# Band biases in natural order added by VectorE, and TensorE's work reordered in two attentions

## The reference, cut to what matters

```python
# first attention: 8 heads, causal
s = jnp.where(k_pos[None, :] <= q_pos[:, None], q @ k.T * scale, NEG_INF); out = softmax(s) @ v
# second ("attention 2"): 12 heads in three groups, a band bias for each head, and 4 heads over a memory
logits = jnp.where(valid, q @ k.T + bias_band, NEG_INF_2)
m = jnp.max(logits, -1); p = jnp.exp(logits - m[..., None]); den = jnp.sum(p, -1)
wts = softmax over the three groups of (m + jnp.log(den)); mixed = concat(p @ v / den * wts)
mem_out = softmax(q_mem @ k_mem.T * scale) @ v_mem
out = concat([mixed, mem_out]) @ w_out
```

## Time and profile before

| | |
|---|---|
| three timed runs, median (lowest to highest) | 2144.69 us (2143.53 to 2150.32) |
| the profiled execution's own time | 2137.23 us |
| its span in the profile | 2135.1 us |
| TensorE matmul, busy | 1900.5 us (89%) |
| VectorE, busy | 585.2 us (27%) |
| ScalarE, busy | 409.5 us (19%) |
| mean granted clock of TensorE | 0.956 |
| transfers | 574.46 MB, mean 269 GB/s |

### The profile page before, as it was taken

The page is one execution under the profiler, slowest core; times in us unless marked ns, Lnnn a source line. Parts: engine busy times, 40 slices in busy tenths (PEclk is TensorE's granted clock), DMA queues, the critical chain, the costliest instruction groups (busy, mean ns, idle before and its releaser), DMA issues.

```text
span 2135.1 us, 24595 instructions
## 1 busy us (share of the span) xinstructions
PE 1900.5 (89%) x9841; PEld 1054.0 (49%) x9842; DVE 585.2 (27%) x1155; ACT 409.5 (19%) x596; POOL 60.9 (3%) x82
## 2 busy tenths in 40 slices
PE   6989997899998887889788779989999999999998
PEld 4645452233332222223232238558884677768863
DVE  4657242211222111212222122331000289520001
ACT  2220222121212122112211221120000334220000
POOL 2000010000000000000000010003001000000000
PEclk9999998999999899999999889999999999999999
DMA  9654758999999999999999992084440423074420
GB/s 317 230 187 171 263 205 354 427 427 391 419 428 428 428 428 427 428 420 390 428 428 428 428 399 102 0 306 130 144 150 22 140 79 129 1 286 149 141 84 20
DMA packets 106225, 574.46 MB, mean 269 GB/s; under 512 B 7271, under 2 KB 8803, under 8 KB 81552
## 3 DMA queue, kind: packets, MB, share of 16 engines
q1 hardware_dynamic: 102000, 563.46, 66.0%
q0 software_dynamic: 4160, 10.06, 1.7%
HBM read 572.42 MB, written 1.07 MB: 269 GB/s over the span
## 4 chain that ended last, share of the span: by engine, by line
PE 72%; DMA 15%; DVE 5%; ACT 4%; issue 2%; SPq 1%; DVEq 0%; ACTq 0%
DMA ring<-in_w_up 14%; PE ps L2073 13%; PE ps L1468 10%; PE ps L2079 7%; PE ps L1503 5%; PE ps L711 5%; PE ps L1482 3%; PE ps L1515 3%; PE ps L897 2%; PE ps L1492 2%; PE ps L2052 2%; PE ps L2175 1%; PE ps L2601 1%; PE ps L1022 1%; DMA ring<-in_w_in 1%
## 5 line engine op out<-in xcount | busy, mean ns | idle before, releaser
L2073 PE MATMUL ps<-arena,ring 128*128 128x256 f32 x1280 | 276.6, 379 | 0.0
L2073 PEld LDWEIGHTS ps<-arena,ring 128*128 128x128 f32 x1280 | 243.6, 190 | 32.4
L1503 PE MATMUL ps<-ring,arena 128*32 128x512 f32 x1216 | 164.5, 690 | 62.1 <-DMA ring<-in_w_up 62.0
L1468 PE MATMUL ps<-ring,arena 128*64 128x512 f32 x960 | 213.1, 596 | 0.0
L2079 PE MATMUL ps<-ring,arena 128*128 128x512 f32 x352 | 151.4, 592 | 0.0
L711 PE MATMUL ps<-arena,ring 128*128 128x256 f32 x608 | 132.8, 380 | 0.0
L1468 PEld LDWEIGHTS ps<-ring,arena 128*64 128x64 f32 x960 | 66.2, 137 | 134.2 <-issue 133.9
L1503 PEld LDWEIGHTS ps<-ring,arena 128*32 128x32 f32 x1216 | 39.8, 125 | 173.4 <-issue 102.6
L711 PEld LDWEIGHTS ps<-arena,ring 128*128 128x128 f32 x608 | 115.3, 190 | 16.7 <-issue 1.6
L1482 PE MATMUL ps<-ring,arena 128*64 128x512 f32 x480 | 106.3, 595 | 11.2 <-ACT arena L1431 11.2
L2079 PEld LDWEIGHTS ps<-ring,arena 128*128 128x128 f32 x352 | 67.0, 190 | 83.2 <-issue 83.1
(11 more groups left out here) (615 smaller groups left out, 2069.8 us busy)
## 6 DMA issues: line engine op xcount, KB each, us to landing
ring<-in_w_gate SPq DMA_DIRECT2D x64, 2048.0 KB, 19.2
ring<-in_w_up SPq DMA_DIRECT2D x64, 2048.0 KB, 22.1
ring<-in_w_down SPq DMA_DIRECT2D x64, 2048.0 KB, 20.3
ring<-in_ffn_w_gate_up SPq DMA_DIRECT2D x22, 2048.0 KB, 8.6
ring<-in_ada_w SPq DMA_DIRECT2D x12, 2048.0 KB, 12.6
ring<-in_ffn_w_down SPq DMA_DIRECT2D x10, 2048.0 KB, 8.0
ring<-in_w_in SPq DMA_DIRECT2D x8, 2048.0 KB, 21.7
ring<-in_dn_w_in SPq DMA_DIRECT2D x6, 2048.0 KB, 7.8
```

The lines of the kernel that those rows point to most:

```text
L1468: m = pe.matmul(bank(b)[c * CAP:(c + 1) * CAP, :], xT[:, j * P + h * CAP:j * P + (h + 1) * CAP], w[h][:, j, c * 512:(c + 1) * 512], start= ...
L1503: m = pe.matmul(bank(b)[(2 * i + c) * FEW:(2 * i + c + 1) * FEW, :], xT[:, j * P + h * CAP:j * P + h * CAP + FEW], w[h][:, j, c * 512:(c + ...
L2073: m = pe.matmul(bank(b0 + g)[:, c * SEQ:(c + 1) * SEQ], w[:, k, (2 * g + c) * P:(2 * g + c + 1) * P], hT2[:, k, :], start=(k == 0), stop=( ...
```

## The change

**Biases.** SyncE copies `band_bias` to a new DRAM tensor `band_rows`, each head's row 128 times. Read with a step of one row less one value, it gives every query its window in natural order, so no flip is needed. VectorE scales the scores and adds the bias (`added`), then takes the maximum and its negative (`top`); ScalarE subtracts it as the bias of its exponential, one head at a time, and sums in the same pass. VectorE's sum goes away. Units 9 to 11 and their banks are interleaved with the rest by hand, and the memory values stand between the scores.

**First attention.** Scores run two units ahead, inside the wait for ScalarE's copy (`meanwhile`); gate 2 comes ahead of the conditioning rows, these stand in unit 2's wait, and the first drive in unit 3's.

**Memory units.** Both are transposed, into different banks, ahead of both value groups.

```diff
+        def sp_bias_rows(sp):
+            sp.wait_ge(bv_stored, 16 * 3)
+            src = bass.AP(bv_dram.tensor, bv_dram.offset, [[2 * SEQ, ATT_HEADS], [0, P], [1, 2 * SEQ]])
+            sp.dma_start(bv_rows, src).then_inc(sp_stored, 16)
...
         def sp_s7(sp):
             for i in range(SLOTS):
                 used = pieces[FIRST - SLOTS + i]
+                if i == SLOTS - 1:
+                    sp_bias_rows(sp)
                 sp.wait_ge(used[1], used[2])
                 load_in(sp, i, 0)
...
         def pool_s9(pool):
             pool.wait_ge(pos_ready, 1)
+            pool.wait_ge(sp_stored, 16)
...
-                        src = bass.AP(bv_dram.tensor, bv_dram.offset + (HPG * g + a) * 2 * SEQ + SEQ - (t + 1) * P,
-                                      [[1, P], [2 * 2 * SEQ, 2], [1, SEQ]])
+                        src = bass.AP(bv_rows.tensor, bv_rows.offset + (HPG * g + a) * P * 2 * SEQ + SEQ - 1 - t * P,
+                                      [[2 * SEQ - 1, P], [2 * P * 2 * SEQ, 2], [1, SEQ]])
...
-                for a in range(2):
-                    pe.matmul(bank(2 * (u % 2) + a), con("flip"), bias[:, 2 * a:2 * a + 2, :], start=True, stop=False, skip_group_check=True)
...
-        def pe_probs(pe, u, n, v_of):
+        def pe_probs(pe, u, n, v_of, meanwhile=lambda: None):
...
             m.then_inc(prT_ps, 1)
+            meanwhile()
             pe.wait_ge(prT_ready, n + 1)
...
+            def late_rows():
+                pe.wait_ge(gate_ready, 3)
+                pe_ada2(pe, 0, 7)
             scores(0)
+            scores(1)
             for u, (g, t) in enumerate(U1):
-                if u + 1 < len(U1):
-                    scores(u + 1)
...
-                if u == 2:
-                    pe_ada2(pe, 0, 7)
-                else:
-                    pe_gate(pe, min(u, 2), 7)
-                pe_probs(pe, u, u, lambda kb, i: vN[:, kb, (HPG * g + i) * HD:(HPG * g + i + 1) * HD])
+                if u < 3:
+                    pe_gate(pe, u, 7)
+                pe_probs(pe, u, u, lambda kb, i: vN[:, kb, (HPG * g + i) * HD:(HPG * g + i + 1) * HD], (late_rows, before_values)[u - 2] if u > 1 else
+                         lambda: scores(u + 2))
...
-        def pe_mem_probs(pe, i):
-            for t in range(TT):
-                pe_probs(pe, MU[i] + t, MU[i] + t, lambda kb, i_: vm[:, kb, i_ * HD:(i_ + 1) * HD])
+        def pe_mem_probs(pe):
+            for n in (4, 5):
+                pe_probs_turned(pe, n, turned_bank(n), 1)
+            for n in (4, 5):
+                pe_probs_values(pe, n, lambda kb, i_: vm[:, kb, i_ * HD:(i_ + 1) * HD])
...
+        def score_bank(n):
+            return 0 if n == 11 else 2 * (n % 2)
+        def turned_bank(n):
+            return 4 - 2 * (n % 2)
...
+            for n in (6, 7, 8):
+                scores(n)
+            pe_mem_values(pe, 1, 5, 0)
+            scores(9)
+            pe_mem_values(pe, 1, 5, 1)
+            scores(10)
+            scores(11)
...
+            turn(6)
+            turn(7)
+            values(6)
+            turn(8)
+            values(7)
+            values(8)
+            ws = [arrived(pe, pc) for pc in pc_ao[0]]
+            pe.wait_ge(ps_read, SQ + 6)
+            pe.wait_ge(pv_ev, 9)
+            out_of(0, 0, 0, KD)
+            turn(9)
+            out_of(0, 1, 0, KD).then_inc(first_ps, 1)
+            turn(10)
+            values(9)
+            turn(11)
+            values(10)
+            values(11)
             pe.wait_ge(pv_ev, 12)
...
+            def exps_less_top(n):
...
+                for h in range(HPG):
+                    o(act.activation(s3[:, h, :], s3[:, h, :], ACT.Exp, bias=nmx[t][:, g, h:h + 1], accum_out=dn3[t][:, g, h:h + 1]),
+                      sc_exp if h == HPG - 1 else None)
...
-                for g in range(3):
-                    n = 6 + 3 * t + g
-                    dve.wait_ge(sc_exp, n + 1)
-                    o(dve.tensor_reduce(dn3[t][:, g, :], heads(n), AX.X, ALU.add))
+                dve.wait_ge(sc_exp, 9 + 3 * t)
                 dve.wait_ge(fn_done, t + 2)
...
+                o(dve.scalar_tensor_tensor(heads(n), bank(score_bank(n), 2).rearrange("p (h k) -> p h k", h=HPG), HD ** -0.5, BM[t][g],
+                                           ALU.mult, ALU.add), ps_read)
+            def top(n):
+                t, g = (n - 6) // 3, (n - 6) % 3
+                o(dve.tensor_reduce(mx3[t][:, g, :], heads(n), AX.X, ALU.max))
+                o(dve.tensor_scalar(nmx[t][:, g, :], mx3[t][:, g, :], -1.0, None, ALU.mult), sc_sub)
...
+            added(6)
+            added(7)
+            top(6)
+            added(8)
+            top(7)
+            top(8)
+            tops(0)
+            added(9)
+            top(9)
+            added(10)
+            weigh(0)
+            top(10)
+            added(11)
+            top(11)
+            tops(1)
+            outs(0)
+            weigh(1)
+            outs(1)
```

More of the change, by code:

```diff
@@ L58, in shape_constants @@
     c["zero_rows"] = np.zeros((P, P))
-    c["flip"] = np.eye(P)[::-1] * HD ** 0.5
     half = HD // 2
@@ L802, in probs_of, with pe_scores @@
             return prob6[n - 6] if 6 <= n < 12 else prob[n % 2]
-        def pe_scores(pe, u, q_of, k_of, bias=None):
-            if bias is not None:
-                for a in range(2):
-                    pe.matmul(bank(2 * (u % 2) + a), con("flip"), bias[:, 2 * a:2 * a + 2, :], start=True, stop=False, skip_group_check=True)
+        def pe_scores(pe, u, q_of, k_of, b0=None):
+            if b0 is None:
+                b0 = 2 * (u % 2)
             for i in range(HPG):
-                m = pe.matmul(bank(2 * (u % 2) + i % 2)[:, (i // 2) * SEQ:(i // 2 + 1) * SEQ], q_of(i), k_of(i), start=bias is None, stop=True,
-                              skip_group_check=bias is not None)
+                m = pe.matmul(bank(b0 + i % 2)[:, (i // 2) * SEQ:(i // 2 + 1) * SEQ], q_of(i), k_of(i), start=True, stop=True)
             m.then_inc(sc_ps, 1)
@@ L874, in act_probsT @@
                 act.wait_ge(pv_ps, n - 1)
-            o(act.copy(prT[n % 2], bank(4, 2)), prT_ready)
+            o(act.copy(prT[n % 2], bank(b0, 2)), prT_ready)
         U1 = [(g, t) for g in range(HEADS // HPG) for t in range(TT)]
@@ L954, in gate_bank, with pe_drive @@
             return 4 + (i + 1) % 2
[L956 to L972 removed]
+        def pe_drive(pe, q):
+            if q:
+                pe.wait_ge(ps_read, q)
+            else:
+                pe.wait_ge(sc_sub, len(U1))
+            for n, (now, last) in enumerate(((BTr, BLr), (BTi, BLi))):
+                at_ = n * HALF
+                for j in range(4):
+                    pe.matmul(bank(j)[:, at_:at_ + HALF], now[32 * j:32 * j + 32, q, :],
+                              uT[32 * j:32 * j + 32, q, :].rearrange("p (s r) -> p r s", r=2)[:, 0, :],
+                              start=True, stop=False, tile_position=(32 * j, 0), skip_group_check=True)
+                for j in range(4):
+                    m = pe.matmul(bank(j)[:, at_ + 1:at_ + HALF], last[32 * j:32 * j + 32, q, :],
+                                  uT[32 * j:32 * j + 32, q, :].rearrange("p (s r) -> p r s", r=2)[:, 1, 0:HALF - 1],
+                                  start=False, stop=True, tile_position=(32 * j, 0), skip_group_check=True)
+            m.then_inc(bu_ps, 1)
+        def pe_s3(pe):
             def gate(i):
@@ L994, in y_of @@
                 m.then_inc(y_ps, 1)
-            drive(0)
             gate(3)
-            drive(1)
+            pe.wait_ge(pv_ev, len(U1))
+            pe.wait_ge(mod_read, 5)
+            pe_drive(pe, 1)
             gate(4)
             y_of(0)
-            drive(2)
+            pe_drive(pe, 2)
             gate(5)
             y_of(1)
-            drive(3)
+            pe_drive(pe, 3)
             gate(6)
@@ L2016, in block_kernel @@
         mxx = [ar(9216 + 40 * t + 36, HPG) for t in range(TT)]
+        nmx = [ar3(9296 + 12 * t, 12, 3) for t in range(TT)]
         actF = ar3(10240, FC2 * SEQ, FC2)
@@ L2177, in out_of, with turn, values @@
                 return m
-            for g in range(3):
-                pe_probs(pe, 6 + g, 6 + g, values_of(g))
-            for g, part in enumerate(((0, 0, KD), (1, 0, KD // 2), (1, KD // 2, KD))):
-                pe_probs_turned(pe, 9 + g)
-                if g == 0:
-                    ws = [arrived(pe, pc) for pc in pc_ao[0]]
-                    pe.wait_ge(pv_ev, 9)
-                    pe.wait_ge(sc_sub, 12)
-                m = out_of(0, *part)
-                if g == 2:
-                    m.then_inc(first_ps, 1)
-                pe_probs_values(pe, 9 + g, values_of(g))
+            def turn(n):
+                if n == 7:
+                    pe.wait_ge(ps_read, SQ + 4)
+                pe_probs_turned(pe, n, turned_bank(n), 1)
+            def values(n):
+                pe_probs_values(pe, n, values_of((n - 6) % 3))
+            turn(6)
[15 more added lines that the diff above has]
+            values(11)
```

(2 more changed lines are left out.)

114 lines of the change are left out of this document (52 added, 62 removed).

## The result

The changed kernel has a median of **2122.7 us** (2112.33 to 2124.36, four runs), against 2147.48 (2143.53 to 2150.32, four runs) for the kernel before: a ratio of 0.9879, 95% interval [0.9852, 0.9905]. It is 25 us faster by the medians, 26 by the ratio; 2120.8 were predicted. Measured again as an experiment it gave the same ratio, 0.9879 [0.9863, 0.9894].

A forecast was written before the change was run, and what follows sets the result against it. TensorE carries 72% of the chain and transfers of expert weights 15%, so waits removed from TensorE outside the experts shorten the run. 10.3 + 2.2 + 11.4 = 23.9 us off the median 2144.69 gives 2120.8; range 2112 to 2133.

The forecast's parts named there:

- First attention, 10.3 us: First attention: regrouped TensorE work starts gate 3 at 147.9 instead of 158.43 us; 10.3 us after 0.2 for handovers.
- It reaches the end: Up to the experts no transfer is on the chain; the expert stream starts and ends 10.3 us sooner.
- The prediction's own sign of being wrong: Wrong if last experts' end to first feed-forward isn't 13 to 14 us shorter, or experts 1, 2 wait longer for weights.
- The copy at nothing: First expert's loads: the 3.15 MB DRAM copy, 8.2 us at 385 GB/s, hides in 16 us of free transfer engines.
- one engine, 131 us: Rival: the copy runs on one transfer engine of 16 at 24 GB/s, 131 us, ending at 2236; chance 0.03.
- Memory units, 2.2 us: Memory units: both transposes first, second values at once behind the first; end 1330.7 instead of 1332.92, 2.2 us.
- Band units, 11.4 us: Attention 2: the output projection's second tile starts at 1412.5 instead of 1423.94 us, 11.4 us sooner.
- The projection starts there: Output projection: starts at 1389.9 us, when both output weights have landed, 16.2 us after the memory values end at 1373.7.
- The low clock: Output projection: its first records run at the lower clock after a sparse stretch, costing 1.7 us (8.77 less 7.07).
- unit 8's copy stands behind unit 10's exponentials on ScalarE: Attention 2: unit 8's copy waits until 1384.7 and takes 1.0 us more; its values end at 1387.
- TensorE waits there for VectorE: Kernel before, 1392 to 1400 us, ahead of the output projection: TensorE waits while VectorE sums and weighs every unit.
- The base: Whole run: the 23.9 us are taken off the timed median, 2144.69, giving 2120.8; off the profiled 2137.23, 2113.3.

The follow-up runs named there:

- four copies: Kernel before with the copy of the bias rows made four times, unused: 2166.86 us against 2145.16, ratio 1.0098.

## Why the prediction was right

**First attention, 10.3 us: right, 10.7.** Both causes were as put: the other work fills the waits for copies, and the conditioning weights are there in time, so that the rows run at 7.07 us.

**It reaches the end: right, by the timed runs.** Alone the first attention gave 11.2 us of the run, 8.4 to 14.2. From the second expert's first issue to the end of the stream are 910.4 to 915.0 us in the thirteen profiles without four copies, 911.8 before, so the stream adds or takes up to 3 us of its own. Ahead of it the clock hides part of the gain in a single profile: gate 3 to that issue took 167.5 to 171.9 us in the five with the old first attention and 169.2 to 175.3 in the eight with the new. Whether the new order makes the low clock there more frequent is not decided. The prediction's own sign of being wrong did not come: from the last expert's last group (1261.18 before, 1261.00 after) to the first feed-forward (1437.78, 1424.29) are 13.3 us less, and between 320 and 440 us TensorE waits for weights for 3.6 us, 4.4 before.

**The copy at nothing: right, with the wrong rate.** I took 385 GB/s and 8.2 us; it runs at 306 GB/s for 10.3 us. Both fit the gap of 16 us. (The 10.3 is 3.15 MB at 306 GB/s; the copy's landing is in no view.) A share of 0.79 where full loads show 1.02 to 1.04 is 0.77 of theirs, near 12 engines of 16 (0.75); which engines carried it no view shows. The Trainium skill (DMA: Bandwidth & Descriptors, Rules for kernel authors) says that an outermost dimension below 16 confines a DMA to at most that many engines. By that the copy was estimated at 10.9 us, and the trace agrees with it rather than with 8.2. The rival "one engine, 131 us" was a rate that no run showed.

**Memory units, 2.2 us: right in their stretch, 2.26.** Timed alone they gave 4.7 us, 2.4 to 7.1, so perhaps more than their stretch; where the rest came from is not shown (above).

**Band units, 11.4 us: right, 11.2 and 11.1** in the two profiles of the changed kernel (62.04 less 50.81 and less 50.98). The step that carried the number, "The projection starts there" at the landing of the output weights, held: 16.5 us behind the issue (16.2 said), waiting for a transfer. The low clock cost 1.6 us where 1.7 stood, priced from another place; in the five profiles with the 2.30 us hold it cost 1.5 to 2.3, so the close agreement is partly luck.

**What was wrong in it did not matter for the sum.** "unit 8's copy stands behind unit 10's exponentials on ScalarE" is true, but the second holder, VectorE's read of unit 6 out of the bank that unit 8's values need, was missed. I had VectorE's passes up to the weighing and its read of unit 8, but put the reads of units 6 and 7 nowhere. ScalarE's unit was 2.53 us and not 2.35: 510 ns for 256 columns from on-chip memory where I took 474 from a row that reads PSUM. Both errors lay under the weights' landing, with 1.5 us of slack. And "TensorE waits there for VectorE", of the 17 us ahead of the projection in the kernel before, holds for the first wait alone, 2.43 us until unit 6 is weighed; the three behind it, 1.14 to 1.15 each, were for ScalarE's copies, and four of the short groups took twice their time at the low clock. No term of the sum rests on it.

**The base: right.** The sum of 23.9 was taken off the median, 2144.69, and not off the profiled execution. The profiled pair shows only 13 us, since the profiled execution of before was early: its unit 0 began at 104.59, those of all other profiles at 105.5 to 110.2. And the way from there to the second expert's first issue differs by the clock too: 327.63 - 104.59 = 223.0 us before, 325.85 - 107.36 = 218.5 after, 4.5 us apart where 10.7 were spared; in 240 to 330 us the clock was 0.92 in the one and 0.85 in the other. Over the profiles this way takes 221.7 to 227.4 us with the old first attention (five, without that of four copies) and 212.3 to 218.5 with the new (eight): the one before is the second shortest of its kind, the one after among the longest.

**Do the parts add up?** First attention 10.7, memory units 2.3, band units 11.2: 24.2 us, for 26.0 measured, 22.7 to 29.4. The parts timed alone add up to more, 11.2 + 4.7 + 14.2 = 30.1; each is uncertain by 2 to 3 us, so the 4 us too many are within the noise. The clock pattern behind the second tile would account for them: the bands alone and the memory units alone have shorter ones (708.5 and 707.2 us to the end), both together the longer (711.3 to 711.6), as before. That it did is not shown.

## What to carry to other kernels

Work put into an engine's waits was worth here what the timeline showed, since what follows is paced by that engine; check it at the next stage that waits for something else, as the output weights did here. When an engine's list is reordered, write down every reader that frees a bank, not only the producers: two holders that end within 0.3 us of each other look like one until the first is gone. And measure from a landmark to a landmark, in more than one profile, since a stretch of 170 us shifted here by 6 us, and one of 710 by 4, through the clock without a changed instruction in it.

## What was not expected of the hardware

- Behind attention 2 the low stretches fall in a few patterns: from the second tile to the end 711.0 to 711.6 us in six profiles, 708.2 to 709.2 in six and 707.1 to 707.2 in two, for the same work. The two kernels profiled twice gave the same length again within 0.4 us.
- A hold of 2.30 us on TensorE amid short groups went with a fall to 0.50, the 1.2 GHz level, at its end or within 2 us of it (1.5 to 2.3 us lost in the projection's first half, five profiles; in three of them 2.11 to 2.79 us of waiting for weights followed); with the hold gone the clock stayed at 1.00 (one profile). In the profile with an idle time of 4.95 us ahead of the transposes the fall came within it, and was over at the projection.
- A DRAM to DRAM copy with 12 rows outermost moved 306 GB/s at a share of 0.79, where weight loads move 385 at 1.02.
